# First attention's weighted sums: natively in fp32, two heads of a pair on the two column halves of TensorE

## The reference

```python
s = jnp.einsum('bqhd,bkhd->bhqk', qb, k).astype(jnp.float32) * scale
s = s + (cq[..., :, None] - cum[..., None, :])
p = masked_softmax(s, causal_mask(start, S))
return jnp.einsum('bhqk,bkhd->bqhd', p.astype(v.dtype), v)
```

## Time and profile before

| what | value |
|---|---|
| three runs | 1445.93, 1451.8 and 1452.55 us, median 1451.8 |
| profiled execution | 1448.33 us, its span 1446.5 us |
| granted TensorE clock, mean | 0.968 |
| TensorE, weight loads | busy 1344.8 us, 1049.3 us |
| VectorE, ScalarE | busy 836.6 us, 579.0 us |
| first attention's steps | 80.64 to 314.21 us |

### The profile page before, as it was taken

One profiled execution on the slowest core, in us unless ns is written; L12 is line 12 of the kernel. 1 busy time (PEld: TensorE's weight loads), 2 busy tenths in 40 slices (PEclk: granted clock), 3 DMA queues, 4 the chain that ended last, 5 costly groups with the idle time before them and its releaser, 6 DMA issues.

```text
span 1446.5 us, 19974 instructions
## 1 busy us (share of the span) xinstructions
PE 1344.8 (93%) x6615; PEld 1049.3 (73%) x6615; DVE 836.6 (58%) x1393; ACT 579.0 (40%) x1043; POOL 12.5 (1%) x27
## 2 busy tenths in 40 slices
PE   5799999979999999999999788888989999999996
PEld 2577777747676888888867566666758888888885
DVE  2646666544655666653336688786566666664323
ACT  4444444433423333322223466664344444432222
POOL 2000000000000000000000100000000000000000
PEclk8799999999899999999999899999989999999998
DMA  9522121264666433333353111111333333333331
GB/s 346 179 96 59 45 64 53 81 234 127 214 236 237 153 99 90 101 95 93 94 155 98 26 28 28 32 36 44 92 112 99 90 101 95 93 100 93 94 95 68
DMA packets 224289, 154.64 MB, mean 107 GB/s; under 512 B 28637, under 2 KB 214450, under 8 KB 220146
## 3 DMA queue, kind: packets, MB, share of 16 engines
q1 hardware_dynamic: 224242, 154.01, 34.3%
HBM read 151.89 MB, written 2.10 MB: 106 GB/s over the span
## 4 chain that ended last, share of the span: by engine, by line
PE 77%; DVE 7%; issue 5%; ACT 5%; DMA 4%; SPq 1%; ACTq 0%; DVEq 0%
PE pj L1312 67%; DMA ada_w_sb<-in_ada_w_dram 3%; PE ov L1535 2%; PE tr L1502 2%; DVE nmax L1006 2%; PE sc L1485 1%; ACT wh L555 1%; ACT tmp L642 1%; PE sc L1375 1%; DMA first_ada<-in_ada_w_dram 1%; PE sc L1381 1%; DVE tmp L1230 1%; DVE wl L888 1%; ACT tmp L825 1%; PE sc L1472 0%
## 5 line engine op out<-in xcount | busy, mean ns | idle before, releaser
L1312 PE MATMUL pj<-hh,wh 128*128 128x512 f32 x1000 | 406.8, 407 | 34.5 <-DVE wl L888 10.2
L888 DVE TENSOR_TENSOR wl<-raw,wh 128x1024 fp32r<-128x1024 f32 (+2 forms) x215 | 235.9, 1097 | 340.5 <-ACT wh L555 339.3
L555 ACT ACTIVATE wh<-raw 128x1024 fp32r<-128x1024 f32 (+2 forms) x215 | 205.6, 956 | 494.4 <-PE pj L1312 493.7
L1312 PE MATMUL pj<-hh,wl 128*128 128x512 f32 x1000 | 394.5, 395 | 0.0
L1312 PE MATMUL pj<-hl,wh 128*128 128x512 f32 x1000 | 394.4, 394 | 0.0
L1312 PEld LDWEIGHTS pj<-hh,wh 128*128 128x128 f32 x1000 | 190.7, 191 | 93.0 <-issue 24.0
L1312 PEld LDWEIGHTS pj<-hh,wl 128*128 128x128 f32 x1000 | 190.5, 191 | 41.1
L1312 PEld LDWEIGHTS pj<-hl,wh 128*128 128x128 f32 x1000 | 191.2, 191 | 36.0 <-issue 0.2
L1312 PE MATMUL pj<-gh,wh 128*128 128x512 f32 x512 | 202.8, 396 | 6.7 <-DVE gl L1033 2.7
L1312 PE MATMUL pj<-gl,wh 128*128 128x512 f32 x512 | 200.8, 392 | 0.0
L1312 PE MATMUL pj<-gh,wl 128*128 128x512 f32 x512 | 200.8, 392 | 0.0
(11 more groups left out here) (179 smaller groups left out, 1286.8 us busy)
## 6 DMA issues: line engine op xcount, KB each, us to landing
raw<-in_ffn_w_in_dram SPq DMA_DIRECT2D x88, 512.0 KB, 3.8
ada_w_sb<-in_ada_w_dram SPq DMA_DIRECT2D x36, 1024.0 KB, 6.0
raw<-in_ffn_w_out_dram SPq DMA_DIRECT2D x32, 448.0 KB, 3.4
raw<-in_fox_w_in_dram SPq DMA_DIRECT2D x24, 512.0 KB, 3.8
first_ada<-in_ada_w_dram SPq DMA_DIRECT2D x8, 1024.0 KB, 9.4
raw<-in_ffn_w_out_dram SPq DMA_DIRECT2D x16, 512.0 KB, 3.6
first_ada<-in_ada_w_dram SPq DMA_DIRECT2D x1, 4096.0 KB, 24.4
raw<-in_fox_w_o_dram SPq DMA_DIRECT2D x8, 512.0 KB, 3.6
```

The costliest lines, as they stand in the source:

```text
L555: act.activation(wh[:, n0 % 2, 0:kt, :], raw[:, n0 % 2, 0:kt, :], ACT.Copy).then_inc(w_hi, 1)
L888: dve.tensor_tensor(wl[:, n0 % 2, 0:kt, :], raw[:, n0 % 2, 0:kt, :], f32(wh[:, n0 % 2, 0:kt, :]), ALU.subtract).then_inc(w_lo, 1)
L1312: ins = pe.matmul(bank_[:, :], (wl if term == 2 else wh)[:, s, kt, :], (rl if term == 1 else rh)(kt), start=start and j == 0, stop=stop an ...
```

## The change

The transposed probabilities are kept once, in fp32, in a buffer `soft` that lies where the low parts lay; v likewise in `v32`, in its last piece. ScalarE alone takes the transposes of probabilities (semaphore `p_out`), VectorE alone takes v (`v_out`). The weighted sum is one fp32 matmul for a block of keys and a head, with a stationary operand of 64 columns, head 0 into rows 0 to 63 and head 1 into rows 64 to 127 of one bank `OV[0]`; so `pair_take` is one instruction on each engine. The second attention keeps its code, with its counts on `tr_hi`, `tr_lo` and `pv` shifted.

```diff
+        def pt32(h, b):
+
+            o, step = (b * P, S) if h == 0 else ((QB - b) * S, S + P)
+            return soft[:, o:o + step * (b + 1)].rearrange("p (k s) -> p k s", s=step)[:, :, 0:P]
+
+        v32 = soft[:, 9 * S:10 * S]
...
+            def fox_turned(h, b, r, bk):
+
+                act.wait_ge(tr_r, r + 1)
+                act.activation(pt32(h, b),
+                               TR[bk][:, 0:(b + 1) * P].rearrange("p (k q) -> p k q", q=P), ACT.Copy
+                               ).then_inc(p_out, 1)
+
             def pair_take(t):
 
-                act.wait_ge(pv, t + 1)
-                for h in range(2):
-                    ins = act.activation(tile(gh, t)[rows_of(h), :], OV[h][rows_of(h), :], ACT.Copy)
-                ins.then_inc(o_hi, 1)
+                act.wait_ge(pv, 2 * t + 2)
+                act.activation(tile(gh, t), OV[0][:, :], ACT.Copy).then_inc(o_hi, 1)
...
                     for v in halves(w - 1):
-                        turned(v % 2, v % 8 // 2, R + fox_turn(v), fox_turn(v) % 2)
-                if w < 8 and d == 1:
-                    act.wait_ge(tr_r, R + (FOX_TR * j + 3))
-                    act.activation(v_all(gh), TR[FOX_TR * j % 2][:, :], ACT.Copy).then_inc(tr_hi, 1)
+                        fox_turned(v % 2, v % 8 // 2, R + fox_turn(v), fox_turn(v) % 2)
...
                 dve.wait_ge(o_hi, t + 1)
-                for h in range(2):
-                    ins = dve.tensor_tensor(tile(gl, t)[rows_of(h), :], OV[h][rows_of(h), :],
-                                            f32(tile(gh, t)[rows_of(h), :]), ALU.subtract)
-                ins.then_inc(o_lo, 1)
+                dve.tensor_tensor(tile(gl, t), OV[0][:, :], f32(tile(gh, t)), ALU.subtract).then_inc(o_lo, 1)
...
-                if w or not first(i):
-                    for v in halves(w - 1):
-                        turned(v % 2, v % 8 // 2, R + fox_turn(v), fox_turn(v) % 2)
                 if w < 8 and d == 1:
-                    dve.wait_ge(tr_hi, R + (FOX_TR * j + 3))
-                    dve.tensor_tensor(v_all(gl), TR[FOX_TR * j % 2][:, :], f32(v_all(gh)),
-                                      ALU.subtract).then_inc(tr_lo, 1)
+                    dve.wait_ge(tr_r, R + (FOX_TR * j + 3))
+                    dve.tensor_copy(v32, TR[FOX_TR * j % 2][:, :]).then_inc(v_out, 1)
...
+            def fox_free(r):
+
+                if r >= 2:
+                    if (r - 2) % FOX_TR == 2:
+                        pe.wait_ge(v_out, took_v(r - 1))
+                    else:
+                        pe.wait_ge(p_out, took_p(r - 1))
...
-            def pair_weighted(r_last):
-
-                pe.wait_ge(tr_lo, r_last + 1)
-                for h in range(2):
-                    for kb in range(QB):
-                        o = pt_off(h, kb, kb)
-                        n = S - kb * P
-                        for term in range(3):
-                            ins = pe.matmul(OV[h][:, kb * P:S], v_all(gl if term == 2 else gh)[:, kb * P:(kb + 1) * P],
-                                            (gl if term == 1 else gh)[:, o:o + n],
-                                            start=kb == 0 and term == 0, stop=kb == QB - 1 and term == 2)
-                ins.then_inc(pv, 1)
+            def pair_weighted(t):
+
+                pe.wait_ge(p_out, 8 * t + 8)
+                pe.wait_ge(v_out, t + 1)
+                for kb in range(QB):
+                    for h in range(2):
+                        o = pt_off(h, kb, kb) - PT0
+                        ins = pe.matmul(OV[0][rows_of(h), kb * P:S],
+                                        v32[:, kb * P + h * HD:kb * P + (h + 1) * HD],
+                                        soft[:, o:o + S - kb * P], start=kb == 0, stop=kb == QB - 1)
+                        if kb == QB - 1:
+                            ins.then_inc(pv, 1)
```

More of the change, by code:

```diff
@@ L147, in build @@
             first_ada = room
+        with nc.sbuf_tensor("below", [P, 2 * DT * S + FFT * S + DT * S], F32):
+            with nc.sbuf_tensor("soft", [P, 10 * S], F32) as room:
+                soft = room
         hh = sb("hh", [P, DT, S], F32R)
@@ L265, in turned_unit, with took_p, took_v @@
             return None if first(i) and s < 2 else s - 2
+        def took_p(r):
+            return r - (r + 6) // FOX_TR
+        def took_v(r):
+            return (r + 6) // FOX_TR
         def done_head(i, s):
@@ L326, in build @@
         tr_lo = sem("tr_lo")
+        p_out = sem("p_out")
+        v_out = sem("v_out")
         pv = sem("pv")
@@ L652, in o_take @@
             def o_take(h, t, hd):
-                act.wait_ge(pv, hd + 1)
+                act.wait_ge(pv, hd + (PAIRS + 1))
                 rows = slice(h * HD, (h + 1) * HD)
                 act.activation(tile(gh, t)[rows, :], OV[h][rows, :], ACT.Copy).then_inc(o_hi, 1)
+            def fox_turned(h, b, r, bk):
[3 more added lines that the diff above has]
+                               ).then_inc(p_out, 1)
             def pair_take(t):
-                act.wait_ge(pv, t + 1)
-                for h in range(2):
-                    ins = act.activation(tile(gh, t)[rows_of(h), :], OV[h][rows_of(h), :], ACT.Copy)
-                ins.then_inc(o_hi, 1)
+                act.wait_ge(pv, 2 * t + 2)
+                act.activation(tile(gh, t), OV[0][:, :], ACT.Copy).then_inc(o_hi, 1)
             def fox_step(i, w, fill, nxt):
@@ L1019, in turned @@
             def turned(h, b, r, bk):
-                dve.wait_ge(tr_hi, r + 1)
+                dve.wait_ge(tr_hi, r - (R_MLA - 1))
                 dve.tensor_tensor(pt_view(gl, h, b), TR[bk][:, 0:(b + 1) * P].rearrange("p (k q) -> p k q", q=P),
@@ L1261, in mla_step @@
                 if s < 8 and b == 3:
-                    dve.wait_ge(tr_hi, R + (MLA_TR * j + 2))
+                    dve.wait_ge(tr_hi, R + (MLA_TR * j + 2 - R_MLA))
                     dve.tensor_tensor(v_half(gl, j), tr_half((R_MLA + MLA_TR * j + 1) % 2),
@@ L1495, in pe_wait_used, with turn @@
                     pe.wait_ge(expd, unit - 1)
-            def turn(u, unit, r, bk, h, b):
+            def turn(u, unit, r, bk, h, b, free):
                 pe.wait_ge(pn, unit + 1)
-                tr_free(r)
+                free(r)
                 for kb in range(b + 1):
@@ L1507, in tr_free @@
             def tr_free(r):
-                if not isinstance(r, int) or r >= 2:
-                    pe.wait_ge(tr_lo, r - 1)
+                if not isinstance(r, int) or r >= R_MLA + 2:
+                    pe.wait_ge(tr_lo, r - (R_MLA + 1))
+            def fox_free(r):
[4 more added lines that the diff above has]
+                        pe.wait_ge(p_out, took_p(r - 1))
             def weighted(h, r_last):
-                pe.wait_ge(tr_lo, r_last + 1)
+                pe.wait_ge(tr_lo, r_last - (R_MLA - 1))
                 for kb in range(QB):
@@ L1584, in fox_step @@
                     for v in halves(w - 1):
-                        turn(v, i * 16 + (U_FOX + v), R + fox_turn(v), fox_turn(v) % 2, v % 2, v % 8 // 2)
+                        turn(v, i * 16 + (U_FOX + v), R + fox_turn(v), fox_turn(v) % 2, v % 2, v % 8 // 2,
+                             fox_free)
                 if fill:
@@ L1592, in fox_step @@
                 if d == 0 and (w or not first(i)):
-                    pair_weighted(R + fox_turn(2 * w - 1))
+                    pair_weighted(i * 2 + j - 1)
                 if w < 8 and d == 1:
                     pe.wait_ge(ev_d, t0)
-                    tr_free(R + (FOX_TR * j + 2))
+                    fox_free(R + (FOX_TR * j + 2))
                     for q in range(QB):
@@ L1714, in mla_step @@
                     r = MLA_TR * (v // QB) + tr_at(v % QB)
-                    turn(v, t * 8 + (U_MLA + v), R + r, (R_MLA + r) % 2, v // QB % 2, v % QB)
+                    turn(v, t * 8 + (U_MLA + v), R + r, (R_MLA + r) % 2, v // QB % 2, v % QB,
+                         tr_free)
                 h = done_head(t, s)
```

## The result

| | median us | lowest to highest | runs |
|---|---|---|---|
| before | 1451.9 | 1445.9 to 1452.6 | 4 |
| changed | 1427.5 | 1425.3 to 1430.7 | 4 |

The ratio is 0.9843, 95% interval [0.9807, 0.9878]: the change makes the kernel faster by 1.6%. The forecast was 1427.6.

The account below looks back on a forecast made before the run. TensorE, busy 93% of the span, was taken as the bound. Gains of 11.7 + 8.2 + 0.8 + 1.3 = 22.0 us, subtracted from the four runs' average of 1449.6, gave 1427.6 us, range 1421 to 1438.

Parts of the forecast that it names:

- Part 1: Weighted sums on TensorE: a pair falls from 3.87 to 2.41 us with halves side by side; 11.7 us over eight pairs.
- The rule on loads: Rival in the weighted sums: weight loads of the column halves are not hidden, costing 3.5 to 7 us; 1431 to 1435, chance 0.09.
- Part 2: Mid-pair TensorE wait for VectorE to take q, and the wait for exponentials behind it, both go: 8.2 us.
- Part 3: The two ends: wait for the probabilities' last low half, 0.8 us; output taking before the output projection, 1.3 us.
- The sum: All gains on TensorE added: 11.7 + 8.2 + 0.8 + 1.3 = 22.0 us.
- This stretch only moves.: The modulation parts before the output projection, tied to weight transfers (5.2 us of waits), shift in time with TensorE's work unchanged.
- One after the other: Rival in the weighted sums: the two halves do not overlap, a pair takes 4.54 us; 1444.6, chance 0.07.
- A remaining wait: Rival: the mid-pair wait for q stays because something else holds VectorE or the split; 1435.8, chance 0.10.
- The slower case: Rival in the weighted sums: every change of half pays a layout switch and load; 20.4 us slower, 1470, chance 0.04.
- The named waits: TensorE's stops before the next pair's third weight block until VectorE takes q: 5.5 us in 6 waits.
- the second term: The mid-pair wait for q and the 0.45 us lost behind each: 8.2 us over six.

Follow-up runs that it names:

- old_takers: Changed kernel, but output taken in two pieces on ScalarE and VectorE, and v copied by ScalarE first with VectorE's copy waiting for it: 1435.1 us.
- two_pieces: Changed kernel, but ScalarE and VectorE take the output in two pieces of 64 rows, as before the change: 1428.5 us.
- the other two comparisons: The changed kernel as it is, measured twice more beside the kernel before: 1423.5 and 1425.6 us.
- whole_array: Changed kernel, but each fp32 matmul loads all 128 columns of v and writes its own bank, giving up the two halves: 1442.8 us.
- before_q_first: Kernel before, but in a pair's second step the split and taking of q come ahead of taking the former pair's output: 1445.2 us.
- two_blocks: Changed kernel, but sums issued as two matmuls of head 0, two of head 1, then the last two of each: 1426.0 us.
- head_by_head: Changed kernel with the loops exchanged: four matmuls of head 0, then four of head 1: 1438.7 us.

## Why the prediction was right

- *Part 1, 11.7 us.* The pair took 2.30 + 0.11 (the switch, which lands in the segment ahead) = 2.41 us, the number of the sum. What the modulation rows showed for four column groups held for two of 64 columns. The way the halves stood in the program mattered more than the prediction knew: it never asked about their order, and head after head would have taken 3.86 us and cost the whole term (1438.7). That the alternating order had been chosen is luck as far as the forecast goes.
- *The rule on loads.* The Trainium skill (TensorE: Matmul & The Clock Gate, Part 3) has loads overlap with matmuls in flight only when the row group differs; the same section's opening also lets a load into the background weight buffer go ahead, which the prediction left out. The trace disagrees with the first sentence: the loads of column halves in the same rows cost nothing at any pass from 512 down to 128 columns, since 2.30 us hold 2.13 of streaming, half of an exposed load and the switch out. By the prediction's estimate of that rule the time would have been 1431 to 1435.
- *Part 2, 8.2 us.* Right in size and in place: the six fills became 8.3 us shorter (21.8 to 13.5), and old_takers brings back the same six waits and the same 8.3 us. The margins were 1.2 us for q and 0.9 for the exponentials, forecast 0.9 and 0.6. The three pieces named were v's path through ScalarE, v's subtraction, and the second piece of the output; two_pieces shows that the last one by itself brings no wait for q, which keeps 0.2 us of margin, but that it uses up the margin of the exponentials and costs 1.1 us. The main share, 7.2 us, is v's way through ScalarE with the two pieces behind it; v's subtraction takes VectorE as long as the copy that replaced it (0.69).
- *Part 3, 0.8 and 1.3 us.* The fill ahead of the seventh sum became 0.72 us shorter, and that sum's segment 0.10 more than the others'. The last pair's segment went from 6.64 to 3.82 us, 2.82 less, of which 1.46 is the sum: 1.36.
- *The sum.* 19.3 us until the first modulation part, forecast 7 x 1.46 + 8.2 + 0.8 = 19.2; and 2.8 at the end, forecast 2.8.
- *What was wrong.* "This stretch only moves." Its length changes by up to 7 us from one execution to the next, with the transfers, and with the granted clock, and so the profile after shows 17.7 us of gain where the medians show 24.4. That is part of the spread of the runs, on both sides, and the median's nearness to 1427.6 is better than the method deserves: the forecast took 22.0 us from 1449.6, the medians have 24.4 from 1451.9, and the two differences cancel. In the other two comparisons (1423.5 and 1425.6 beside 1448.2 and 1448.0) the gain is 24.7 and 22.5 us.
- *The rivals.* One after the other (forecast 4.5 us and 1444.6) is what whole_array does: 4.41 and 1442.8. A remaining wait (1435.8) is what old_takers does: 1435.1. The slower case, each change of half as a change of layout, did not occur in any run. The named waits of the kernel before (5.5 us) understate the second term by a third; what the fill lost behind the named wait had to be read from segment lengths.

## What to carry to other kernels

Where a stationary operand has only 64 columns, give the two halves of the columns to two independent products and alternate them in the program; the gain (4.4 to 2.3 us here) is lost for the most part when one product's matmuls are all issued first. To price a form that a trace does not contain, look for a relative of it elsewhere in the same trace, here the four-group modulation matmuls. When a stall is to be cured, follow what comes after it on the same engine: in before_q_first the wait only changed its name, while the change shortened the path to the next maxima by 2.2 us, half of it waits for another engine, and freed both.

## What was not expected of the hardware

- TensorE starts a matmul for an idle column half ahead of passes that wait for the other half, but with a short reach: over three waiting passes with their loads (two_blocks, where both halves start within 14 ns; head_by_head, where head 1's first pass starts 6 ns behind head 0's fifth), and not over four or more (head 1 did not start with head 0's first to fourth pass).
- A stretch of eight 1 MB loads through two buffers, with the same code, took 22.9 to 29.9 us in eleven profiles, and its length goes with how long the granted clock lay at 0.50 in it: not at all up to 25.2 us, 6.8 us at 25.6 to 26.6, 10.2 us at 29.9. Such a part takes 1.88 us at 0.50 and 1.04 at 1.00.
